# Streaming encoder layer on one core: late weight units loaded whole instead of in halves

## The chip, the core and the metric

The kernel runs on 1 core of one Trainium2 chip. The core has five engines with instruction streams of their own: TensorE (PE, matmuls), VectorE (DVE), ScalarE (ACT), GpSimd (POOL) and SyncE (SP, which here only issues DMAs). Sixteen DMA engines move data between HBM and the on-chip memory. The metric is the device time of one execution in microseconds; less is better.

## The reference

One transformer-like layer for 640 tokens (512 prompt tokens, and 8 streams of 16 sample tokens), D = 2048, all in float32:

```
p  = x @ w_in                              # q, k, v and gates of two mixers
h  = LN1(alpha*x + (sigmoid(gA)*(yA@w_proj_a) + sigmoid(gB)*(yB@w_proj_b)) @ w_out)
q  = h @ w_query                           # 8 heads, product keys, top 16 of 128 x 128
y  = LN2(alpha*h + sum_k gate_k * gelu(u[e_k] . h) * v[e_k])   # PEER, 16384 experts
```

`yA` and `yB` are two kinds of band attention. The part that matters here is PEER. The tables `u` and `v` are 16384 x 2048 floats each.

## The kernel before

**Weights as units.** Every stationary matrix is cut into units of 128 x 2048 floats (1 MB) that stand one behind another in `wstream`. SP loads unit n into `raw[n % 2]`; there are two such buffers. To keep float32 accuracy a unit is split: `w_hi` is the unit rounded to the matmul's format, and `w_lo = raw - w_hi`. PE then computes three products for each pair of tiles (high x high, low x high, high x low).

**Two stages.** Up to unit U_LATE the split is made by POOL alone and each unit is loaded whole (`raw_full`). The 240 units from U_LATE on, which this text calls late, are split in halves of 1024 columns: ACT rounds a half (`split_high`, L1024 to L1027), POOL subtracts it (`low`, L325 to L330), and each half is also loaded by a DMA of its own (L308 to L320).

**The order of one late unit n** (buffer s = n % 2). ACT's first half of `w_hi[s]` waits until PE has read the first half of unit n - 2 (`half_read`, or `part_done` where the unit holds `v`), and until the half has landed. POOL's `low` of half 0 raises `low_first`; its `low` of half 1 raises `split_done`. Between and behind the two lows POOL issues the gathers that are written out for this position. ACT's second half waits for the end of unit n - 2 on PE (`unit_done`).

**SP's queue.** It is in order. Half 0 of unit n + 2 may be loaded when `low_first` says that half 0 of unit n has been read, and half 1 when `split_done` says so for half 1.

**Where the halves are used.** 384 tokens go through PEER densely on PE: for each group of 4 x 128 experts, 4 units of `u` (`act_step`, L642), gelu, times the gate matrix, then 4 units of `v` (`out_units`, L706), whose results DVE adds into `r_acc` (L1439). The other 256 tokens go through PEER sparsely: POOL gathers 128 rows of 8 KB (1 MB, L365) from `u_rows` or `v_rows` into one of four buffers, and DVE multiplies and sums them (L1412, L1415), then frees the buffer (`rows_used`, which POOL waits for at L358 and L359). 16 early units of `u` come before U_LATE, and their results are kept in HBM.

**Trips.** First run 4 mixed trips, each with 12 late units (4 of `u`, 8 of `v`), 32 gathers and two loads of gates; then 24 late groups of 8 units, 16 gathers and one load of gates. A load of gates (L1031, issued by ACT) brings 768 KB of the gate matrix into `G4`; DVE's `product` (L1425) of the group waits for it. DVE works in program order: a product that waits holds back the gathered rows behind it, and so POOL's next gathers.

**Queues.** SP's loads run on DMA queue 1, POOL's gathers on queue 0, ACT's loads of gates on queue 10.

The functions that the change touches, and what calls them:

Of the kernel before, what the change touches and what calls it, by code (L numbers as in the profile page):

```python
# [50 lines left out]
U_LATE = U_PEER + N_EARLY  # L51
HALVES = (slice(0, D // 2), slice(D // 2, D))
# [30 lines left out]
def build(nc, x_t, wstream, u_rows, v_rows, cka, cva, ckb, cvb, rext, negs, bp_b, bs_b, sinks, lnp, lnrow, subk, consts, pt_out, y_out, n_out):  # L83
# [3 lines left out]
    ds = bass.ds  # L87

    with ExitStack() as ctx:
# [3 lines left out]
        def sb(name, shape, dt=f32):  # L93
            return ctx.enter_context(nc.sbuf_tensor(name, shape, dt))

        def sem(name):
            return ctx.enter_context(nc.semaphore(name))
# [9 lines left out]
        raw = [sb(f"w_raw{s}", [P, D]) for s in range(2)]  # L107
# [95 lines left out]
        def cut(ap, h):  # L203
# [10 lines left out]
                      lambda z, h=h: banks[:, 2 * z + h, 0:HALF]) for h in range(2)],  # L214
# [5 lines left out]


        raw_full = [sem(f"raw_full{s}") for s in range(2)]
        raw_half = [[sem(f"raw_half{s}_{h}") for h in range(2)] for s in range(2)]
        half_read, low_first = sem("half_read"), sem("low_first")
        hi_done, hi_late, split_done, unit_done = sem("hi_done"), sem("hi_late"), sem("split_done"), sem("unit_done")

# [72 lines left out]
        @block.sync  # L299
        def _(sp):  # L300
            for s in range(2):
                sp.dma_start(raw[s][:, :], wstream[s]).then_inc(raw_full[s], 16)
            with sp.Fori(1, U_LATE // 2) as i:
                for s in range(2):
                    sp.wait_ge(split_done, 2 * i + s - 1)
                    sp.dma_start(raw[s][:, :], wstream[ds(2 * i + s, 1)].rearrange("a p c -> p (a c)")) \
                        .then_inc(raw_full[s], 16)
            for s in range(2):  # L308
                sp.wait_ge(split_done, U_LATE - 1 + s)
                for h, half in enumerate(HALVES):  # L310
                    sp.dma_start(raw[s][:, half], wstream[U_LATE + s][:, half]).then_inc(raw_half[s][h], 16)
            with sp.Fori(1, (UNITS - U_LATE) // 2) as i:
                for s in range(2):
                    for h, half in enumerate(HALVES):
                        if h == 0:
                            sp.wait_ge(low_first, 2 * i + s - 1)
                        else:
                            sp.wait_ge(split_done, U_LATE - 1 + 2 * i + s)
                        sp.dma_start(raw[s][:, half], wstream[ds(U_LATE + 2 * i + s, 1), :, half].rearrange("a p c -> p (a c)")) \
                            .then_inc(raw_half[s][h], 16)  # L320


        @block.gpsimd
# [438 lines left out]
        def _(act):  # L762
# [204 lines left out]
            with act.Fori(0, N_QUERY // 2) as i:  # L967
                for s in range(2):
                    c = 2 * i + s
# [53 lines left out]

            def split_high(s, pair, h):  # L1024

                act.wait_ge(raw_half[s][h], 16 * pair + 16)
                act.activation(w_hi[s][:, HALVES[h]], raw[s][:, HALVES[h]], ACT.Copy).then_inc(hi_late, 1)  # L1027

            def load_gates(g, q):
# [13 lines left out]
            def act_units(g, q, first):  # L1043
                load_gates(g, q)
                for e in range(EG):
                    act.wait_ge(half_read, 4 * (g - EARLY) + e + 1)
                    split_high(e % 2, (first - U_LATE) // 2 + 1 + e // 2, 0)
                    act.wait_ge(unit_done, first + e + 1)
                    act.activation(banks[:, e, 0:N2], banks[:, e, 0:N2], ACT.Gelu).then_inc(gelu_done, 1)
                    split_high(e % 2, (first - U_LATE) // 2 + 1 + e // 2, 1)  # L1050
                    high_part(q, e, 0, banks[:, e, 0:N2])

            def out_unit(q, first, v):
                act.wait_ge(part_done, 12 * q + 3 * v + 2)
                split_high(v % 2, (first - U_LATE) // 2 + 1 + v // 2, 0)
                act.wait_ge(unit_done, first + v + 1)
                split_high(v % 2, (first - U_LATE) // 2 + 1 + v // 2, 1)
# [64 lines left out]
        def _(dve):  # L1122
# [127 lines left out]
            def layer_norm(q, between=None):  # L1250
                wide = [(cols, [out(z) for z in range(2)]) for (src, cols, out) in ln_parts[q]]
                dve.wait_ge(ln[q]["sum"], 1)
                for cols, out in wide:
                    last = dve.tensor_scalar(mean_t[:, cols], out[0], 1.0 / D, None, ALU.mult)
                own.done(last)
                own.wait()
                parts = ln_parts[q] if q else [(lambda k: Rt[:, k, :], slice(0, T), None)]
                for k in range(KT_N):
                    for (src, cols, _) in parts:
                        last = dve.tensor_tensor(src(k), src(k), mean_t[:, cols], ALU.subtract)  # L1260
                    last.then_inc(ln[q]["centered"], 1)
                if between:
                    between()
                dve.wait_ge(ln[q]["sq_used"], KT_N)
                for cols, out in wide:
                    last = dve.tensor_scalar(rstd_t[:, cols], out[1], 1.0 / D, EPS, ALU.mult, ALU.add)
                last.then_inc(ln[q]["var"], 1)
                dve.wait_ge(ln[q]["std"], 1)
                own.done(dve.reciprocal(rstd_t[:, cols], rstd_t[:, cols]) if q else dve.reciprocal(rstd_t, rstd_t))
                own.wait()  # L1270
                dve.wait_ge(ln[q]["centered"], KT_N)
                for k in range(KT_N):
                    for (src, cols, _) in parts:
                        last = dve.scalar_tensor_tensor(src(k), src(k), lnt[:, 2 * KT_N * q + k:2 * KT_N * q + k + 1],
                                                        rstd_t[:, cols], ALU.mult, ALU.mult)
                    last.then_inc(ln[q]["scaled"], 1)
                    if q == 0 and k:
                        split_shifted(k - 1)
# [371 lines left out]
```

## Time and profile before

| what | us |
| --- | --- |
| median of 3 runs | 4903.42 |
| lowest, highest | 4902.08, 4904.24 |
| the profiled execution, its own time | 4904.37 |
| its span, first to last instruction | 4902.6 |
| PE busy | 4388.6 |
| POOL busy | 2597.2 |
| DVE busy | 2675.2 |
| mean granted TensorE clock | 0.959 |

The profiled execution took 4904.37 us, of which 4902.6 us is the span that the rows below are measured in. Busy time is a sum over the whole program, whose stages differ.

### The profile page before, as it was taken

How to read it: one execution, taken by the hardware profiler on the slowest of the kernel's cores; microseconds unless marked ns; L12 is line 12 of the kernel's file. 1: busy time of each engine (PE TensorE's matmuls, PEld its weight loads, DVE VectorE, ACT ScalarE, POOL GpSimd, SP SyncE). 2: the span in 40 equal slices, each digit the busy share in tenths (PEclk: the TensorE clock that was granted, in tenths of full speed). 3: DMA queues.
4: the chain of work that ended last, by engine and by line, in shares of the span. 5: the costliest groups of instructions: out<-in, count | busy, mean ns of one | idle time of the engine just before them, and what ended most of it. 6: DMA issues, size and time to landing. Idle time of an engine off the chain costs nothing.

```text
span 4902.6 us, 74877 instructions
## 1 busy us (share of the span) xinstructions
PE 4388.6 (90%) x26508; PEld 4190.5 (85%) x26508; DVE 2675.2 (55%) x4819; ACT 1065.1 (22%) x1872; POOL 2597.2 (53%) x1718
## 2 busy tenths in 40 slices
PE   8999999999899989858867887999989999999996
PEld 8999888888799979857767777898889899998985
DVE  1000333344423138988966666766667667666667
ACT  1000222222311011012222222222223323322222
POOL 4454222232254534433266665767767777777673
PEclk9999999999999999979988989999999999999998
DMA  5222232222332321113478888889889899898895
GB/s 195 98 96 101 107 124 106 93 80 82 121 119 102 101 71 52 68 53 142 163 305 345 342 326 346 347 332 357 341 343 367 334 362 358 340 356 345 327 355 225
DMA packets 265955, 1081.84 MB, mean 221 GB/s; under 512 B 24496, under 2 KB 89136, under 8 KB 181168
## 3 DMA queue, kind: packets, MB, share of 16 engines
q0 software_dynamic: 74736, 544.24, 27.7%
q1 hardware_dynamic: 87840, 388.01, 21.7%
q10 hardware_dynamic: 103328, 148.96, 8.8%
q8 instruction: 25, 0.41, 0.0%
q14 instruction: 26, 0.21, 0.0%
HBM read 1019.65 MB, written 66.85 MB: 222 GB/s over the span
## 4 chain that ended last, share of the span: by engine, by line
PE 50%; DMA 17%; DVE 14%; issue 12%; POOL 5%; ACT 1%; DVEq 1%; ACTq 1%; POOLq 0%
PE banks L464 28%; PE banks L706 13%; DMA work<-gate_matrix 8%; DMA rows_own<-in_v_rows,idx 3%; POOL w_lo L329 3%; DMA rows_own<-in_u_rows,idx 2%; DVE banks L1415 2%; PE banks L642 2%; DMA work<-in_u_rows,idx 2%; POOL work L365 2%; PE banks L694 2%; PE banks L533 2%; PE banks L495 1%; DVE work L1412 1%; PE banks L503 1%
## 5 line engine op out<-in xcount | busy, mean ns | idle before, releaser
L329 POOL TENSOR_TENSOR w_lo<-w_raw,w_hi 128x1024 fp32r<-128x1024 f32 x480 | 1159.1, 2415 | 373.2 <-ACT w_hi L1027 367.5
L335 POOL TENSOR_SCALAR w_hi<-w_raw 128x2048 fp32r<-128x2048 f32 x130 | 253.5, 1950 | 1485.6 <-PE banks L464 1270.0
L464 PE MATMUL banks<-mv_hi,w_hi 128*128 128x256 f32 x3648 | 864.1, 318 | 61.9 <-DVE mv_lo L1134 38.0
L706 PE MATMUL banks<-mv_hi,w_hi 128*128 128x384 f32 x2048 | 723.5, 353 | 212.5 <-DVE work L1439 135.7
L464 PE MATMUL banks<-mv_lo,w_hi 128*128 128x256 f32 x3648 | 836.8, 311 | 0.0
L464 PE MATMUL banks<-mv_hi,w_lo 128*128 128x256 f32 x3648 | 835.6, 310 | 0.0
L642 PE MATMUL banks<-mv_hi,w_hi 128*128 128x384 f32 x2048 | 704.6, 344 | 77.8 <-POOL w_lo L329 61.7
L464 PEld LDWEIGHTS banks<-mv_hi,w_hi 128*128 128x128 f32 x3648 | 652.5, 189 | 125.9 <-issue 102.3
L1027 ACT ACTIVATE w_hi<-w_raw 128x1024 fp32r<-128x1024 f32 x480 | 506.2, 1057 | 968.7 <-PE banks L706 764.3
L706 PE MATMUL banks<-mv_lo,w_hi 128*128 128x384 f32 x2048 | 711.6, 347 | 0.0
L706 PE MATMUL banks<-mv_hi,w_lo 128*128 128x384 f32 x2048 | 710.5, 347 | 0.0
L642 PE MATMUL banks<-mv_lo,w_hi 128*128 128x384 f32 x2048 | 692.3, 338 | 0.0
L642 PE MATMUL banks<-mv_hi,w_lo 128*128 128x384 f32 x2048 | 691.8, 338 | 0.0
L339 POOL TENSOR_TENSOR w_lo<-w_raw,w_hi 128x512 fp32r<-128x512 f32 x520 | 679.2, 1337 | 10.9
L464 PEld LDWEIGHTS banks<-mv_lo,w_hi 128*128 128x128 f32 x3648 | 670.2, 190 | 0.0
L464 PEld LDWEIGHTS banks<-mv_hi,w_lo 128*128 128x128 f32 x3648 | 669.5, 189 | 0.0
L706 PEld LDWEIGHTS banks<-mv_hi,w_hi 128*128 128x128 f32 x2048 | 405.1, 198 | 241.2 <-DVE work L1439 149.7
L1415 DVE SCALAR_TENSOR_TENSOR banks<-work,subkt,banks 128x2048 f32<-128x2048 f32 x192 | 451.1, 2349 | 275.2 <-DMA work<-gate_matrix 234.4
L1412 DVE CUSTOM_DVE_ANT_0 work<-work,banks 128x2048 f32<-128x2048 f32 x192 | 438.2, 2282 | 242.8 <-DMA work<-gate_matrix 136.1
L642 PEld LDWEIGHTS banks<-mv_hi,w_hi 128*128 128x128 f32 x2048 | 391.0, 191 | 88.4 <-POOL w_lo L329 50.9
L706 PEld LDWEIGHTS banks<-mv_lo,w_hi 128*128 128x128 f32 x2048 | 405.9, 198 | 0.0
L706 PEld LDWEIGHTS banks<-mv_hi,w_lo 128*128 128x128 f32 x2048 | 405.0, 198 | 0.0
(159 smaller groups left out, 4825.5 us busy)
## 6 DMA issues: line engine op xcount, KB each, us to landing
w_raw<-in_wstream SPq DMA_DIRECT2D x480, 512.0 KB
w_raw<-in_wstream SPq DMA_DIRECT2D x130, 1024.0 KB, 4.8
gate_matrix<-work ACTq DMA_DIRECT2D x12, 2048.0 KB, 6.3
work<-gate_matrix ACTq DMA_DIRECT2D x32, 768.0 KB
out_p<-work ACTq DMA_DIRECT2D x34, 320.0 KB, 2.2
work<-out_p ACTq DMA_DIRECT2D x34, 320.0 KB, 3.4
gate_scratch<-work ACTq DMA_DIRECT2D x32, 320.0 KB, 2.2
work<-gate_scratch ACTq DMA_DIRECT2D x16, 640.0 KB, 3.9
```

The source lines that it names most:

```text
L329: pool.tensor_tensor(w_lo[s][:, part], raw[s][:, part], w_hi[s][:, part].bitcast(f32), ALU.subtract) \
L335: pool.tensor_scalar(w_hi[s][:, :], raw[s][:, :], 1.0, 0.0, ALU.mult, ALU.add).then_inc(hi_done, 1)
L339: last = pool.tensor_tensor(w_lo[s][:, part], raw[s][:, part], w_hi[s][:, part].bitcast(f32), ALU.subtract)
L365: pool.indirect_dma_start(rows_t[c % ROWS], None, table, bass.IndirectOffsetOnAxis(ap=idx2[:, c % 16:c % 16 + 1], axis=0)) \
L464: last = pe.matmul(acc(dst, h), a[s][:, P * k:P * k + P], b[h][:, k, :], start=(k == k_first and n == 0), stop=(k == k_last and n == 2))
L533: last = pe.matmul(o, v_nat[:, P * kb + HD * hh:P * kb + HD * hh + HD], pt[:, P * c:P * c + P], start=(c == 0), stop=(c == nk - 1))
L642: last = pe.matmul(banks[:, bank, 0:N2], a[s][:, P * k:P * k + P], b[1][:, k, :], start=(k == 0 and n == 0), stop=(k == KT_N - 1 and n == 2))
L694: last = pe.matmul(banks[:, 2 + q % 2, P * t:P * t + P], oh2[:, n, :].bitcast(f32), oh1[:, n, :], start=True, stop=True)
L706: last = pe.matmul(banks[:, d, 0:N2], a[v % 2][:, at:at + P], b[z][:, e, :], start=(e == 0 and n == 0), stop=(e == EG - 1 and n == 2))
L1027: act.activation(w_hi[s][:, HALVES[h]], raw[s][:, HALVES[h]], ACT.Copy).then_inc(hi_late, 1)
L1412: ins = dve.tensor_tensor_reduce(rows, rows, nat, 1.0, 0.0, ALU.mult, ALU.add, dots[:, c:c + 1])
L1415: ins = dve.scalar_tensor_tensor(nat, rows, act_n[:, ds(col + c, 1)], nat, ALU.mult, ALU.add)
```

## The change

SP issues one DMA of 1 MB for each late unit, where it issued two of 512 KB. The one DMA waits for `split_done`; SP no longer waits for `low_first`, which PE still uses. The two semaphores of a buffer's halves become one, `raw_late`, and both halves of ACT's rounding wait for it. Rounding, subtraction and what they release stay in halves. The first two late units are loaded whole too.

```
-        raw_half = [[sem(f"raw_half{s}_{h}") for h in range(2)] for s in range(2)]
+        raw_late = [sem(f"raw_late{s}") for s in range(2)]
...
             for s in range(2):
                 sp.wait_ge(split_done, U_LATE - 1 + s)
-                for h, half in enumerate(HALVES):
-                    sp.dma_start(raw[s][:, half], wstream[U_LATE + s][:, half]).then_inc(raw_half[s][h], 16)
+                sp.dma_start(raw[s][:, :], wstream[U_LATE + s]).then_inc(raw_late[s], 16)
             with sp.Fori(1, (UNITS - U_LATE) // 2) as i:
                 for s in range(2):
-                    for h, half in enumerate(HALVES):
-                        if h == 0:
-                            sp.wait_ge(low_first, 2 * i + s - 1)
-                        else:
-                            sp.wait_ge(split_done, U_LATE - 1 + 2 * i + s)
-                        sp.dma_start(raw[s][:, half], wstream[ds(U_LATE + 2 * i + s, 1), :, half].rearrange("a p c -> p (a c)")) \
-                            .then_inc(raw_half[s][h], 16)
+                    sp.wait_ge(split_done, U_LATE - 1 + 2 * i + s)
+                    sp.dma_start(raw[s][:, :], wstream[ds(U_LATE + 2 * i + s, 1)].rearrange("a p c -> p (a c)")) \
+                        .then_inc(raw_late[s], 16)
...
             def split_high(s, pair, h):
 
-                act.wait_ge(raw_half[s][h], 16 * pair + 16)
+                act.wait_ge(raw_late[s], 16 * pair + 16)
                 act.activation(w_hi[s][:, HALVES[h]], raw[s][:, HALVES[h]], ACT.Copy).then_inc(hi_late, 1)
```

On SP, in the loop over the late units (one pass is two units, one for each buffer), stood before the change and stand now, with the semaphore that a row waits for:

```order
-L319 ISA [waits low_first]
-L319 DMA w_raw<-in_wstream 128x1024
...
-L319 ISA [waits split_done]
-L319 DMA w_raw<-in_wstream 128x1024
-L319 ISA [waits low_first]
-L319 DMA w_raw<-in_wstream 128x1024
-L319 ISA [waits split_done]
-L319 DMA w_raw<-in_wstream 128x1024
...
+L314 ISA [waits split_done]
+L314 DMA w_raw<-in_wstream 128x2048
+L314 ISA [waits split_done]
+L314 DMA w_raw<-in_wstream 128x2048
```

The transfer that waited for `low_first` is gone, and its 1024 columns moved into the one behind `split_done`. No instruction of PE, DVE, ACT or POOL moves.

## Rows read from the trace of the kernel before

**Rows 1.** Windows by stage: length, engines' busy time, clock, DMA share, GB/s

```profile
2467.00:3110.00 643.00, 501.61 (x2607) 489.65 (x2608) 436.60 (x485) 139.76 (x169) 414.54 (x273) 0.89 0.88 338
3110.00:4840.00 1730.00, 1592.61 (x8834) 1566.27 (x8833) 1130.74 (x1072) 484.20 (x572) 1245.59 (x787) 0.98 0.90 347
```

**Rows 2.** PE's groups of instructions from 2467 to 4840 us

```profile
L706 PE MATMUL banks<-mv_hi,w_hi 128*128 128x384 f32 x2021 | 714.4, 353 | 212.5 <-DVE work L1439 135.7 <-DVE mv_lo L1429 76.6
...
L642 PE MATMUL banks<-mv_hi,w_hi 128*128 128x384 f32 x1792 | 608.4, 339 | 74.2 <-POOL w_lo L329 61.7 <-DVE work L1439 12.5
```

**Rows 3.** Chain that ended last, one late group: start, us, what

```profile
4032.56 13.27 DMA work<-gate_matrix
...
4056.37 8.00 DMA work<-in_u_rows,idx
...
4066.99 8.94 DMA rows_own<-in_u_rows,idx
...
4078.76 19.03 PE banks L706 x108
```

**Rows 4.** Windows of that group and of a mixed trip: columns as in rows 1

```profile
4063.00:4089.00 26.00, 21.59 (x122) 20.64 (x121) 19.94 (x24) 7.71 (x9) 22.02 (x16) 1.00 1.01 415
2643.00:2647.00 4.00, 4.00 (x25) 4.00 (x24) 4.00 (x7) 2.80 (x4) 3.83 (x3) 1.00 1.00 418
2639.00:2641.00 2.00, 2.00 (x14) 2.00 (x13) 2.00 (x1) 0.00 (x0) 1.17 (x2) 1.00 0.00 0
4046.00:4050.00 4.00, 4.00 (x25) 4.00 (x24) 3.98 (x3) 0.00 (x0) 0.94 (x2) 1.00 0.02 8
2641.00:2682.00 41.00, 31.21 (x164) 30.25 (x163) 32.66 (x35) 9.49 (x14) 27.35 (x19) 0.91 0.99 399
2720.00:2728.00 8.00, 5.02 (x20) 5.02 (x21) 7.12 (x10) 2.42 (x3) 4.94 (x3) 0.61 0.18 42
```

**Rows 5.** Timeline of SP, narrow windows: start, us, issue of a half

```profile
2635.86 0.33 SPq L319 DMA_DIRECT2D w_raw<-in_wstream  x1
2645.51 0.33 SPq L319 DMA_DIRECT2D w_raw<-in_wstream  x1
4041.32 0.33 SPq L319 DMA_DIRECT2D w_raw<-in_wstream  x1
4052.82 0.33 SPq L319 DMA_DIRECT2D w_raw<-in_wstream  x1
4056.38 0.33 SPq L319 DMA_DIRECT2D w_raw<-in_wstream  x1
4059.93 0.33 SPq L319 DMA_DIRECT2D w_raw<-in_wstream  x1
```

**Rows 6.** DMA queue 1 in 2636:2639, 4044:4046: packets, MB, share

```profile
q1 hardware_dynamic: 143, 0.52, 51.8%
...
q1 hardware_dynamic: 131, 0.49, 66.6%
```

**Rows 7.** Page, DMA issues: size, median us from issue to landing

```profile
w_raw<-in_wstream SPq DMA_DIRECT2D x130, 1024.0 KB, 4.8
```

**Rows 8.** Timelines of ACT and POOL after the gates have landed

```profile
4063.42 1.05 ACT L1027 ACTIVATE w_hi<-w_raw 128x1024 fp32r<-128x1024 f32 x1
...
4066.72 1.06 ACT L1027 ACTIVATE w_hi<-w_raw 128x1024 fp32r<-128x1024 f32 x1 [0.72 <-DMA w_raw<-in_wstream]
...
4067.97 2.41 POOL L329 TENSOR_TENSOR w_lo<-w_raw,w_hi 128x1024 fp32r<-128x1024 f32 x1
4070.54 0.96 POOL L365 DMA_INDIRECT work<-in_u_rows,idx  x1 [0.16 <-issue]
```

**Rows 9.** Timeline of DVE, same stretch

```profile
4080.02 2.28 DVE L1412 CUSTOM_DVE_ANT_0 work<-work,banks 128x2048 f32<-128x2048 f32 x1
```

**Rows 10.** DMA queues from 3200 to 4800 us: packets, MB, share of 16 engines

```profile
q0 software_dynamic: 49287, 358.87, 56.2%
q1 hardware_dynamic: 48814, 177.73, 30.2%
```

## Prediction

> **What bounds the kernel now.** I read the windows by stage first [rows 1]. Before 2467 us only whole units are used and the change touches next to nothing. From there to 4840 us run the 240 late units, with the DMA engines 0.88 to 0.90 busy. In the mixed trips (643 us) PE is busy for only 502 us; in the late groups (1730 us) for 1593 us, so there PE is nearly the bound. What PE waits for stands in its groups [rows 2]: 212.5 + 74.2 = 286.7 us of idle time, of which 148.2 us end with DVE's addition into `r_acc` (L1439), 76.6 us with DVE's low part of the products (L1429), and 61.7 us with POOL's subtraction. No row there names the weight load itself. So the question is not whether PE waits for a load, but what delays DVE and POOL.
>
> The chain that ended last tells that for one late group [rows 3]. The load of gates takes 13.27 us from issue to landing; DVE stands still meanwhile. Then two gathers follow, 8.00 us and 8.94 us from issue to use, and only then PE starts its long run at 4078.76. Each of these is a transfer that shares the 16 DMA engines. Behind the landing the engines are full (4063:4089: share 1.01, 415 GB/s [rows 4]). Only right after it they are idle (4046:4050: 8 GB/s), since DVE has freed no buffer yet and POOL has issued no gather. In a mixed trip it is the same picture, longer: idle at 2639:2641, then 0.99 busy for 41 us. So behind each landing of gates runs a chain whose length is bytes divided by the rate, and PE's stalls end with it.
>
> **The change, part by part.**
>
> *Bytes and instructions.* The bytes stay. SP issues 240 DMAs fewer (0.33 us each), on a queue that nothing else uses and that mostly waits: no gain. The packets of a load grow from 4 KB to 8 KB. In the full windows a mixture of 4 KB packets and 8 KB gathers moves 415 GB/s (4063:4089), gathers alone 418 GB/s (2643:2647) [rows 4]: I price packet size at 0. The nearest row for the other end is the share that each queue's packets took [rows 10]: queue 0 moves 358.87 MB at 56.2%, so queue 1 at that rate would need 27.8% for its 177.73 MB and has 30.2%. 2.4% of the DMA-bound stretches (about 100 of 158 us in each of 4 trips, about 23 of some 72 us, 1730 / 24, in 24 groups, 950 us) is 23 us, the upper bound of a gain.
>
> *The first half leaves later.* It was allowed out after POOL's first low of unit n, now after the second. In a stretch where POOL is not stopped that is 3.5 us later (4056.38 to 4059.93 [rows 5]). But where the gates are awaited, POOL is stopped between the two lows, by a gather whose buffer DVE has not freed: 4041.32 to 4052.82, and 2635.86 to 2645.51 [rows 5]. In the mixed trip the half issued at 2635.86 moved its 0.52 MB in 2636:2639 [rows 6], at a time when no gather was under way, free of charge. Now these bytes are issued at 2645.5, into the full stretch. They lengthen it by 0.52 MB / 0.415 MB per us = 1.26 us. Two landings of gates in each of 4 trips give 8 x 1.26 = **10 us**. Other pauses of the gathers in a trip, as 2720:2728 at 42 GB/s [rows 4], could lose as much, up to 2 more a trip, 10 us; but there DVE waits for its own small loads and PE's next stall begins before the engines are full again, so I take 0 for these.
>
> *The same in a late group.* Here the half issued at 4041.32 overlaps the gates: in 4044:4046 queue 1 moved 0.49 MB [rows 6]. Behind the landing the count up to the chain's second gather, at 4075.9, was 5 1/3 halves (second half of one unit, two units, a third of the next first half); now it is 3 whole units, 6 halves, since the next is issued only after 4074. 2/3 of 0.52 MB is 0.35 MB, 0.85 us longer. Against that the gates land earlier, since that half is no longer among their rivals, while the unit before it is loaded later and gives part of this back; I take 0.5 us of the 1.1 us that 0.49 MB are worth. Net 0.35 us, with ends 0 - 0.25 and 0.85. For 24 groups: **8 us**, ends -6 and 20.
>
> *Is a whole load in time?* Uncontended, 1 MB takes 4.8 us [rows 7], of which 1.05 MB / 0.418 = 2.5 us is moving, so 2.3 us is fixed. Sharing turn by turn with one gather doubles the moving: 2.3 + 5.0 = 7.3 us. The tightest place is the load issued at 4059.93: it would land at 4067.2, where ACT's first half of it was rounded at 4063.42 and the second at 4066.72, the latter already 0.72 us late [rows 8]. Rounding then ends at 4068.3, and POOL's low, which began at 4067.97 because POOL was busy until then, slips by 0.4 us; the next unit by about 0.8. POOL's gathers behind it slip alike. The one issued at 4070.54 [rows 8] is used by DVE at 4080.02 without any wait [rows 9], 9.5 us later, against 8.0 and 8.9 us for the ones in the chain. So 0.4 to 0.8 us is hidden by that queueing time. Price 0. Away from the landings POOL follows PE, a unit every 8.4 us, and the load has about 8.7 us to ACT's first half: also hidden. If this cover were gone, each group would pay the slip.
>
> *Sum.* 4904.4 (this execution's own time) + 10 + 8 = **4922 us**. The profiled execution is 1 us over the median of the runs, 4903.4; I keep 4922.
>
> **The skill on large transfers.** The rows show that a whole load of 1 MB takes 4.8 us alone [rows 7], and that PE's waits name no load [rows 2]. The Trainium skill, page "DMA: Bandwidth & Descriptors", section "Bandwidth", has the rule to batch DMAs to 1 MiB and more, and gives about 2.0 us of fixed cost for each plus the bytes at 436 GB/s; by that two halves cost 6.4 us and one whole 4.4 us, an estimate, and 240 units would give back 480 us if loads were on the path. The rule is for transfers that are waited for one by one; here the trace speaks against a gain of that size, since two halves overlap other transfers.
>
> **Rivals.**
> 1. *Larger packets win* (faster). If the 2.4% of rows 10 is true engine time and the idle-time bytes are recovered in the slack of the steady stretches (0.90 busy on average), the 23 us stand against about 8: 4904 - 15 = 4889. For it: the shares of rows 10. Against: equal rates in the full windows. It decides where windows with whole loads move over 4% more than 415 GB/s.
> 2. *It cancels* (no change). The half that was free in idle time is lost, but the gates' load has fewer rivals and the gathers ahead of the chain fewer bytes to share with; the two terms shrink to 0 to 8 us: 4904 to 4912. For it: in late groups my own net is only 0.35 us out of terms of 0.5 and 0.85.
> 3. *The load is late* (slower still). If a contended whole load takes 9.5 us, 2.2 more than worked out, the slip is 2.6 us and then about 5 at the next unit, past the 1 us or so that queueing hides; gathers and then PE move by about 2 us in each group, 48 us, and the sum is 4970. For it: ACT's second half is already 0.72 us late. Against: 7.3 us is already the case with a gather beside it all the way. It decides from about 8.5 us.
>
> **How the numbers follow.** My forecast (4913 to 4940) gets 0.42, the cancelling 0.31, larger packets 0.14, late loads 0.13. The bounds of the terms alone give 4904 - 6 - 23 = 4875 to 4904 + 20 + 20 = 4944; to leave out no more than 0.2, the range goes from 4892 to 4955. My forecast's own range is 4908 to 4940. 0.2% is 9.8 us, about what a measurement of this kernel tells from no change: faster means under 4893.6, slower over 4913.2. Faster 0.14; within 0.31; slower 0.55.
>
> **What the profile afterwards would show.** (a) The load behind the one that stalls now, near 4041, is issued only when POOL's second low ends, and the DMA engines are idle for longer after each landing of gates, 1 to 2 us more. (b) The mixed stage, 643 us, is about 10 us longer, the late one, 1730 us, about 8. (c) The chain still runs gates, two gathers, PE, with gathers of 8 to 10 us. (d) ACT's wait for `w_raw` is more frequent, once or twice a group, under 1 us at the second half's old place, at most 4 at the first's; POOL's wait for ACT grows, PE's for POOL's subtraction does not. (e) Full windows stay near 415 GB/s. The prediction is wrong if (e) fails upward, if whole loads under contention take over 8.5 us, or if PE's idle time behind L1439 does not grow.

## The result and the profile after

| kernel | median us | lowest to highest | runs |
| --- | --- | --- | --- |
| before | 4905.31 | 4894.05 to 4914.35 | 16 |
| changed | 4875.93 | 4855.65 to 4903.25 | 15 |

The ratio is 0.994, with a 95% interval of 0.9927 to 0.9953: the change makes the kernel 29 us or 0.6% **faster**, where 4922 us was predicted. (Executions far off all others, of 11954.88 us here and of 7710.94 and 7067.46 us of the kernel before in later runs, are left out.) Besides the median the spread moved: 20 us before, 48 us now. The profiled execution of the changed kernel is the slowest of its 15, 4903.25 us, so its trace shows what the change does to the transfers and hardly any of the gain. For the gain I ran the same kernel again (first experiment). All lines from L324 on stand five lower than before: L1434 is what L1439 was.

Windows by stage of the changed kernel [rows 1]: length, busy time of PE, PEld, DVE, ACT and POOL, clock, DMA share, GB/s.

```profile
2469.00:3112.00 643.00, 506.27 (x2629) 493.44 (x2630) 436.51 (x488) 140.15 (x170) 417.41 (x275) 0.89 0.87 339
3112.00:4840.00 1728.00, 1578.62 (x8818) 1549.87 (x8817) 1131.66 (x1070) 483.88 (x571) 1244.37 (x785) 0.98 0.89 347
```

PE's groups of the same stretch [rows 2]:

```profile
L701 PE MATMUL banks<-mv_hi,w_hi 128*128 128x384 f32 x2023 | 710.5, 351 | 231.1 <-DVE work L1434 129.4 <-DVE mv_lo L1424 101.6
L637 PE MATMUL banks<-mv_hi,w_hi 128*128 128x384 f32 x1792 | 607.1, 339 | 63.4 <-POOL w_lo L324 60.6 <-DVE work L1434 2.8
```

The chain that ended last, one late group [rows 3], its long pieces:

```profile
4031.23 13.70 DMA work<-gate_matrix
...
4066.09 9.63 DMA rows_own<-in_u_rows,idx
```

Windows of that group [rows 4]: behind the landing of the gates, and the full stretch after it.

```profile
4045.00:4050.00 5.00, 5.00 (x31) 5.00 (x30) 4.89 (x5) 0.00 (x0) 1.83 (x3) 1.00 0.00 0
4051.00:4069.00 18.00, 17.29 (x98) 16.65 (x97) 13.37 (x16) 6.92 (x11) 15.63 (x11) 1.00 0.99 395
```

The view of SP's line of late loads, x238: who waited for them (us, times), and the time to landing.

```profile
  ACT w_hi L1022: 448.1, 123
...
DMA to landing us min/median/max: 4.6/8.9/11.0
```

DMA queue 1 from 3200 to 4800 us [rows 10]:

```profile
q1 hardware_dynamic: 24340, 177.24, 28.9%
```

Read together: half as many packets on queue 1 for the same bytes, and 28.9% of the engines' time for them instead of 30.2%; an idle stretch of 5 us behind the landing, and a full one at 395 GB/s, not above the 415 of before. The idle stretch is no longer than it was: before, it stands one microsecond later.

```profile
4046.00:4051.00 5.00, 5.00 (x31) 5.00 (x30) 4.98 (x6) 0.00 (x0) 1.92 (x3) 1.00 0.09 16
```

ACT now waits for weights 123 times, 3.6 us each in the mean. And yet PE waits no longer for POOL's subtraction: 60.6 against 61.7 us. In this one execution nothing is won either: it is within 2 us of the kernel before.

### The profile page after: what moved, and what is told of

Read it like the earlier page. It is cut to its first block, busy times and chain, and to the rows that moved or that the text cites. A ratio compares the mean times of both kernels' runs of the same rounds, so it can differ in the third digit from the quotient of the medians.

```text
span 4901.5 us, 74042 instructions
## 1 busy us (share of the span) xinstructions
PE 4380.2 (89%) x26508; PEld 4179.1 (85%) x26508; DVE 2677.4 (55%) x4819; ACT 1065.6 (22%) x1872; POOL 2598.5 (53%) x1718
## 4 chain that ended last, share of the span: by engine, by line
PE 49%; DMA 17%; DVE 14%; issue 12%; POOL 6%; ACT 1%; DVEq 1%; ACTq 0%; POOLq 0%
PE banks L459 28%; PE banks L701 12%; DMA work<-gate_matrix 8%; POOL w_lo L324 4%; DMA work<-in_u_rows,idx 2%; DMA rows_own<-in_u_rows,idx 2%; DMA rows_own<-in_v_rows,idx 2%; DVE banks L1410 2%; PE banks L637 2%; POOL work L360 2%; PE banks L689 2%; PE banks L528 2%; PE banks L490 1%; DMA work<-in_v_rows,idx 1%; DVE work L1407 1%
## 5 line engine op out<-in xcount | busy, mean ns | idle before, releaser
L324 POOL TENSOR_TENSOR w_lo<-w_raw,w_hi 128x1024 fp32r<-128x1024 f32 x480 | 1158.2, 2413 | 367.1 <-ACT w_hi L1022 361.8
L637 PE MATMUL banks<-mv_hi,w_hi 128*128 128x384 f32 x2048 | 704.7, 344 | 67.1 <-POOL w_lo L324 60.6
## 6 DMA issues: line engine op xcount, KB each, us to landing
work<-gate_matrix ACTq DMA_DIRECT2D x32, 768.0 KB, 14.3
```

The source lines that it names most:

```text
L324: pool.tensor_tensor(w_lo[s][:, part], raw[s][:, part], w_hi[s][:, part].bitcast(f32), ALU.subtract) \
L637: last = pe.matmul(banks[:, bank, 0:N2], a[s][:, P * k:P * k + P], b[1][:, k, :], start=(k == 0 and n == 0), stop=(k == KT_N - 1 and n == 2))
```

## Experiments

Each kernel was timed in five rounds against the kernel before on the same chip. Medians of before were 4905 to 4912 us, so the ratios are what is compared; a difference between two kernels is the difference of their ratios times 4904.

| run | median us | ratio | 95% interval |
| --- | --- | --- | --- |
| whole_again | 4868.11 | 0.9916 | 0.9885 to 0.9946 |
| halves_at_second_low | 4889.94 | 0.9965 | 0.9952 to 0.9979 |
| whole_in_trips | 4892.2 | 0.9967 | 0.995 to 0.9984 |
| whole_in_groups | 4874.98 | 0.9944 | 0.9922 to 0.9966 |
| gates_in_6kb_halves | 4798.29 | 0.9781 | 0.9759 to 0.9803 |
| gates_in_6kb_halves_at_second_low | 4789.42 | 0.9758 | 0.9737 to 0.9778 |
| gates_in_6kb_whole | 4763.31 | 0.9708 | 0.9688 to 0.9729 |
| gates_6kb_one_dma_4kb | 4764.28 | 0.97 | 0.9676 to 0.9723 |
| gates_6kb_one_dma_8kb_copy | 4753.49 | 0.9673 | 0.9648 to 0.9698 |
| one_dma_4kb | 4879.54 | 0.9943 | 0.9916 to 0.9971 |
| whole_as_two_dmas | 5524.12 | 1.1252 | 1.1228 to 1.1276 |
| whole_as_four_quarters | 5119.77 | 1.0437 | 1.0413 to 1.0462 |
| early_acts_sooner_halves | 4876.79 | 0.9941 | 0.9925 to 0.9957 |
| early_acts_sooner_halves_late | 4879.95 | 0.9936 | 0.992 to 0.9952 |
| early_acts_sooner_one_dma_4kb | 4864.1 | 0.99 | 0.9868 to 0.9933 |
| early_acts_sooner_whole | 4852.81 | 0.9886 | 0.9867 to 0.9905 |
| gates_6kb_whole_early_acts_sooner | 4751.58 | 0.9677 | 0.9655 to 0.9699 |

Two lengths are used below, both of the profiled execution and both from the issue times of the gates' loads on ACT: *trips* is from the first load to the ninth (the four mixed trips), *group* the mean distance from the ninth to the 32nd, over 23. *DVE for gates* adds the two rows of who waited for those loads.

| run | span | trips | group | DVE for gates |
| --- | --- | --- | --- | --- |
| before | 4902.6 | 584.6 | 75.10 | 370.5 |
| changed, the execution above | 4901.5 | 583.6 | 75.02 | 367.3 |
| whole_again | 4835.1 | 564.2 | 73.23 | 313.1 |
| halves_at_second_low | 4884.5 | 569.9 | 75.18 | 370.5 |
| one_dma_4kb | 4852.8 | 556.7 | 74.18 | 327.7 |
| gates_in_6kb_halves | 4796.5 | 581.1 | 70.65 | 257.0 |
| gates_in_6kb_whole | 4764.3 | 546.1 | 70.72 | 243.2 |
| gates_in_6kb_halves_at_second_low | 4787.7 | 566.9 | 70.86 | 249.3 |
| gates_6kb_one_dma_4kb | 4760.9 | 548.2 | 70.66 | 225.3 |

### The same kernel again

No edit; the changed kernel as it is.

> The changed kernel once more, for its time and for a second profiled execution, since the first profiled execution took 4903 us where the median of the others was 4876 us. Theory A (the larger packets use the DMA engines better): about 4876 us, and in the profile the full windows move more than 415 GB/s. Theory B (the later issue leaves the engines to the gates and the gathers): about 4876 us, with a shorter wait for the gates. If the first profiled execution was only at the slow end of a wide spread, this one is likely to be nearer 4876 us and shows in which stage the time is saved.

Measured: 0.9916, and its profiled execution took 4836.88 us, near the low end of its own spread (4833.49 to 4888.35). The chain that ended last, two groups of it:

```profile
3401.75 7.85 DMA work<-gate_matrix
...
3430.99 10.05 DMA rows_own<-in_v_rows,idx
...
3444.13 25.26 PE banks L701 x144
...
3469.85 14.87 DMA work<-gate_matrix
...
3506.06 9.32 DMA rows_own<-in_v_rows,idx
...
3518.47 26.54 PE banks L701 x144
...
3545.48 8.00 DMA work<-gate_matrix
```

The first load of gates lands in 7.85 us, and the next group begins 68.1 us later; the second takes 14.87 us, and its group 75.6 us. Nothing else in the chain differs by as much. Of the 24 late groups seven have such a landing here, of 7.5 to 8.1 us; in the execution shown above none has, its shortest being 9.3 and 10.3 us. (Three groups, the first, ninth and seventeenth, lie between the two lengths in both.) The two rows of who waited for the gates say what it is worth; of before and of this run:

```profile
  DVE banks L1415: 234.4, 16
  DVE work L1412: 136.1, 10
```

```profile
  DVE banks L1410: 195.4, 16
  DVE work L1407: 117.7, 10
```

57.4 us less waiting. L1415 and L1412 are DVE's steps on gathered rows. In the code DVE's wait for the gates (`act_units` on DVE) stands ahead of the group's first two such steps, which do not read the gates; what that order costs was not tried.

The gates are 768 KB in 1536 packets of 512 bytes. DMA queues (packets, MB, share of 16 engines) in the first group at 3406:3408, and in the second at 3475:3477 and 3477:3479:

```profile
q10 hardware_dynamic: 1074, 0.55, 94.8%
q0 software_dynamic: 17, 0.03, 4.2%
...
q10 hardware_dynamic: 739, 0.38, 65.4%
q0 software_dynamic: 48, 0.27, 32.3%
...
q1 hardware_dynamic: 52, 0.43, 54.9%
q0 software_dynamic: 35, 0.28, 33.7%
q10 hardware_dynamic: 254, 0.13, 25.4%
```

With the other queues empty the gates rush through, over 500 packets a microsecond. Once gathers and weights are back, as in the changed kernel at 4039:4042, each queue gets about as many packets as the other, and the gates a few:

```profile
q1 hardware_dynamic: 76, 0.62, 50.0%
q0 software_dynamic: 74, 0.61, 48.6%
q10 hardware_dynamic: 47, 0.02, 2.8%
```

The packets take turns singly: of the 47 packets of gates 26 are followed, within 3 ns of their end, by the start of a gather's packet and only 6 by another of the gates; by chance it would be 8 and 5. At 16 packets of 512 bytes a microsecond what is left of the gates crawls until the others stop. So the landing has two lengths. That the short one comes where the gap lasts some 3 us, 1536 packets at 500 a microsecond, is my reading of these windows.

### One stage at a time

Of whole_in_trips, with `N_CUT` = 25 (the end of the trips); whole_in_groups has the two bodies the other way round:

```
+            with sp.Fori(1, N_CUT) as i:
+                for s in range(2):
+                    sp.wait_ge(split_done, U_LATE - 1 + 2 * i + s)
+                    sp.dma_start(raw[s][:, :], wstream[ds(U_LATE + 2 * i + s, 1)].rearrange("a p c -> p (a c)")) \
+                        .then_inc(raw_half[s][0], 16)
+                    sp.sem_inc(raw_half[s][1], 16)
-            with sp.Fori(1, (UNITS - U_LATE) // 2) as i:
+            with sp.Fori(N_CUT, (UNITS - U_LATE) // 2) as i:
```

> Whole loads for the 50 units of the mixed trips alone, halves in the late groups. It divides the gain of some 29 us between the stages. Theory A (packets): the gain is in proportion to the time in which the DMA engines are full, about 100 of 158 us in each of 4 trips against 23 of 75 us in 24 groups, so about 12 us of the 29 are here: 4893 us. Theory B (later issue): it goes by landings of gates, 8 of 32, so about 7 us: 4898 us.

> Halves in the mixed trips, whole loads in the late groups alone. Theory A (packets): about 17 us of the 29, 4888 us. Theory B (later issue): about 22 us, 4883 us. Either way this and the run with whole loads in the trips should add up to the whole gain; if they do not, the stages act on one another.

Measured: -16 us and -27 us, whose sum of 43 us is that of whole_again (-41 us), though the first measurement of the whole change gave 29 us. The gain is in both stages. In the profiled executions whole_in_trips has 578.0 and 74.81 us (trips, group), whole_in_groups 591.8 and 73.55.

### The deferral alone

```
                         if h == 0:
-                            sp.wait_ge(low_first, 2 * i + s - 1)
-                        else:
                             sp.wait_ge(split_done, U_LATE - 1 + 2 * i + s)
```

Still two loads of 512 KB in 4 KB packets, both at the second low. This is the step that the prediction priced at 10 + 8 us.

> Two loads of 512 KB as before, but both issued at the end of the second low, when the changed kernel issues its one of 1 MB. This is the later issue alone, with 4 KB packets. Theory A (packets): no faster than before, 4905 us or, if the later issue costs what the prediction said, about 4922 us. Theory B (later issue): about 4876 us like the changed kernel.

Measured: 0.9965, **17 us faster**, in a narrow spread (4886 to 4898). Its group is as long as before, its trips 15 us shorter. Where these come from shows in a mixed trip of the kernel before: timeline of SP, ACT, DVE and POOL, each asked in a window of its own.

```profile
2707.49 0.33 SPq L319 DMA_DIRECT2D w_raw<-in_wstream  x1
...
2708.03 0.93 ACTq L1040 DMA_DIRECT2D work<-early_act  x2
...
2716.54 0.56 DVE L1425 TENSOR_TENSOR work<-work 128x384 f32<-128x384 f32 x1 [5.95 <-DMA work<-early_act]
2720.76 0.56 DVE L1425 TENSOR_TENSOR work<-work 128x384 f32<-128x384 f32 x1 [3.67 <-DMA work<-early_act]
...
2722.90 2.38 POOL L329 TENSOR_TENSOR w_lo<-w_raw,w_hi 128x1024 fp32r<-128x1024 f32 x1 [10.42 <-ACT w_hi L1027]
```

A half goes out half a microsecond ahead of two small loads (192 KB each) for which DVE then stands still 9.6 us. The window of rows 4 at 2720:2728, 42 GB/s, is the end of this: ACT's next rounding stands in its order behind what it makes of DVE's two products, POOL's low waits 10.42 us for that rounding, and the gathers behind the low stop. DVE's whole wait for these loads, before, with the halves deferred, and in whole_again:

```profile
  DVE work L1425: 33.9, 8
```

```profile
  DVE work L1423: 17.9, 8
```

```profile
  DVE work L1420: 22.9, 7
```

### These waits taken away

ACT issues the two small loads ahead of the third output unit instead of behind it:

```
-                out_unit(2 * i, first + EG, 2)
                 for e in range(2, 4):
                     load_act(i, q, e, 8 * i + 7 + e - 2)
+                out_unit(2 * i, first + EG, 2)
```

> The kernel before, but ACT issues the last two loads of early activations of a mixed trip (192 KB each) about 4.7 us sooner, ahead of the rounding of the next unit's first half. Theory D: in the mixed trips the halves loaded at the first low collide with these small loads, for which DVE waits 5.9 and 3.7 us in a trip, while everything else stands still; whole loads, issued later, leave them a free stretch. If they are issued sooner their waits go for halves too: some 4 us for each of the 4 trips, so about 4890 us. If these waits cost nothing in the end, the time stays at 4908 us.

> The changed kernel with the same two loads issued sooner. Theory D: the part of the gain that comes in the mixed trips (16 us) is mostly had already by the sooner loads, so whole against halves gives less than before, 12 to 20 us (the short landings of gates in the late groups) instead of 29 to 40: about 4870 us. If the later issue gains in another way, whole loads keep their whole lead: about 4855 us.

> The kernel before with the small loads of early activations issued sooner (4876.8 us), and now also with both halves of the weights issued at the second low. What the deferral of the first half does is here seen without the waits for early_act that it shortens. If the deferral by itself costs as the prediction had it (1.26 us for each landing of gates in the trips, 0.35 us in a group, 18 us in all), this run is at 4895 us (4885 to 4905). If it costs nothing and all of its 17 us of gain came from the shorter waits, it is at 4877 us (4870 to 4883). Below 4870 us the deferral gains by more than these waits.

> The same early issue of the small loads, the weights as one load of 4 KB packets at the second low, gates in 512 byte packets. One load of 8 KB packets was at 4852.8 us here. If it is one load in place of two that gives the clear run of 3.4 us, this run is at 4853 to 4866 us with some landings of gates under 9 us, and at least 10 us below the run with two halves; if it is the packets' size, it is within 5 us of the run with two halves.

Measured: in halves 0.9941, which is 29 us from an edit that touches no weights, and more than the 15 us or so that I had expected. Deferring both halves on top of it gives 0.9936, the same within the intervals: once the waits for early_act are gone, the deferral neither gains nor costs (-2 us, about +-11). Its trips are 559.6 against 557.7 us. So the 17 us were these waits, and the 18 us of cost that I had computed are not there. The whole load keeps a lead of 27 us over the halves here (0.9886 against 0.9941), so its lead does not rest on these waits alone, and one load of 4 KB packets keeps 18 us over the deferred halves (0.99 against 0.9936); that last pair's intervals overlap.

### The gates in 6 KB packets

The gate matrix is stored in HBM as [group, partition, block, expert x token], so that a load of gates has 128 packets of 6 KB instead of 1536 of 512 bytes. The 12 stores that write the matrix, ahead of the late units, are laid out to match (not shown); each takes 9.1 us to land instead of 6.3.

```
-        G_s = dram("gate_matrix", (GBLK, P, KEYS, GT))
+        G_s = dram("gate_matrix", (GROUPS, P, GBLK, EG * GT))
...
-                act.dma_start(G4.rearrange("p b e t -> p b (e t)"),
-                              G_s[:, :, ds(EG * g, EG), :].rearrange("b p e t -> p b (e t)")).then_inc(g4_in, 16)
+                act.dma_start(W2[:, 2 * N2:6 * N2],
+                              G_s[ds(g, 1)].rearrange("a p b c -> p (a b c)")).then_inc(g4_in, 16)
```

> The kernel before, with the gate matrix laid out in HBM so that a load of gates is 128 runs of 6 KB (8 packets for each DMA engine) instead of 1536 runs of 512 bytes (96 for each); weights in halves as before. Theory C, from the profiles so far: a load of gates is served one packet for each packet of the other queues, so it ends only in a moment when gathers and weights are both drained; whole loads open such a moment now and then, the load of gates then lands in 7 to 8 us instead of 14 to 15, and the group takes 67 us instead of 75. With 8 packets it needs no such moment: landing after 5 to 9 us in every group, about 7 us less for each of 30 loads, so about 4700 us. Theory A (packet size of the weights): the wait for the gates goes by bytes, which are the same, so about 4905 us.

> The changed kernel with the same layout of the gate matrix. Theory C: as fast as with the weights in halves, about 4700 us, less at most the 16 us of the later issue in the mixed trips; the gain of whole loads in the late groups, 27 us, is gone, and the spread of the times is as small as before. Theory A: the 29 us between whole and half stay, wherever the total lies.

> Gates in runs of 6 KB, and both halves issued at the second low. Halves at their old places with these gates took 4798 us, whole loads 4763 us, and the 35 us between them lie in the mixed trips. If they come from the time of issue (theory D), this run takes 4763 to 4775 us; if from the size of the packets, about 4798 us.

Measured: I had expected about 4700 us with halves, and it is 4798. The landing has one length, but not the 5 to 9 us that I had counted on; the row of the gates' load in gates_in_6kb_halves:

```profile
DMA to landing us min/median/max: 4.1/9.9/10.9
```

In halves this takes 107 us off the kernel before, almost four times what the change studied here gives. A group is 70.65 us with halves and 70.72 with whole loads: with the gates in large packets for both, **the change gains nothing in the groups**. Its gain there was the chance of a short landing. The spread went with it in these two runs, 15 and 12 us over five executions; the later kernels with 6 KB gates and one load spread over 24 to 27 us, so the spread has another part that is not explained. In the trips the gain stays, and is larger (581.1 to 546.1); all in all the ratio still falls from 0.9781 to 0.9708, 36 us, of which the deferral gives 11 us (0.9758, between my two expectations) and the rest 25 us.

### What the rest is: packets of 8 KB, or one load instead of two

Two first tries split the whole load again, at the same low. Of whole_as_two_dmas, whose packets stay 8 KB:

```
-                    sp.dma_start(raw[s][:, :], wstream[ds(U_LATE + 2 * i + s, 1)].rearrange("a p c -> p (a c)")) \
+                    for p in (slice(0, P // 2), slice(P // 2, P)):
+                        sp.dma_start(raw[s][p, :], wstream[ds(U_LATE + 2 * i + s, 1), p].rearrange("a p c -> p (a c)")) \
```

> The whole unit at the end of the second low, as two DMAs of 64 partitions each with packets of 8 KB. It tells the number of DMAs from the size of the packets: the halves at the second low were two DMAs with packets of 4 KB and took 4890 us. If the packets count (theories A and C): about 4870 us, with landings of gates in under 10 us in some of the late groups. If the number of DMAs counts: about 4890 us and hardly any.

> The whole unit at the end of the second low, as four DMAs of 512 columns with packets of 2 KB. With packets taken in turns with the gathers a load then takes 32 turns of an engine instead of 8, so the weight queue is hardly ever empty beside gathers. Theory C: no short landing of gates in the late groups, and loads land later (over 10 us beside gathers), so that POOL waits: 4890 us or more. If only the time of issue counted, about 4890 us as with halves, and the same landings.

Both failed as tests. The two loads of 64 partitions each made the kernel 12.5% slower. Its DMA records from 3200 to 4700 us, and those of whole_again:

```profile
DMA packets 81382, 409.90 MB, mean 273 GB/s; under 512 B 8313, under 2 KB 32889, under 8 KB 32889
...
q0 software_dynamic: 36553, 266.22, 59.7%
q1 hardware_dynamic: 19990, 131.01, 31.9%
```

```profile
DMA packets 102736, 537.82 MB, mean 359 GB/s; under 512 B 8288, under 2 KB 39008, under 8 KB 39008
```

The engines were no less busy (95.0% against 92.1% with queue 10's 3.4% and 3.7%), at three quarters of the rate. Four quarters of 512 columns (2 KB packets, four loads) cost 4.4%, with ACT waiting 1474.2 us for weights; that changes size and number at once. My expectation for the number of short landings missed too: half of its groups had one.

Then one load with packets of 4 KB, from a second input `wlate` of the late units, laid out as [unit, half, partition, 1024]; a control has that second input with packets of 8 KB.

```
-                    sp.dma_start(raw[s][:, :], wstream[ds(U_LATE + 2 * i + s, 1)].rearrange("a p c -> p (a c)")) \
+                    sp.dma_start(raw[s][:, :].rearrange("p (h c) -> p h c", h=2),
+                                 wlate[ds(2 * i + s, 1)].rearrange("a h p c -> p (a h) c")) \
```

> The changed kernel, but a late unit's 1 MB comes from a copy of the weights laid out so that its one load has packets of 4 KB where the changed kernel's has 8 KB; one issue, one wait, the same bytes at the same second low. If it is the packets that give the whole load its further 24 us over two halves issued together (4889.9 us), this kernel is at about 4890 us (4880 to 4900), the load takes about 7.5 us from first to last packet beside the gathers (whole in 8 KB packets 5.3 us), and next to none of the gates' loads of the late groups lands in under 9 us. If it is the number of loads (two issues on SyncE against one), it is at about 4870 us (4855 to 4880), with packets of 4 KB or not, and the load takes as long as that of the changed kernel.

> The gates in packets of 6 KB, which takes the chance of the short landings away, and a late unit's 1 MB as one load of 4 KB packets from a second copy. With gates in 6 KB two halves at the second low took 4789.4 us and one load of 8 KB packets 4763.3 us, both in narrow spreads. If the 26 us between them are the packets' size, this run is at 4789 us (4783 to 4795); if they are the number of loads, at 4763 us (4757 to 4770); in between both have a part.

> The control for the run with 4 KB packets: the same second input for the late units, but laid out as before, so that the one load has packets of 8 KB. Both theories expect 4763 us (4757 to 4770), the time of one load of 8 KB packets from the first input. If this run is elsewhere, where the copy lies in HBM has a price of its own and the other run must be read against this one.

Measured: with the gates in 512 bytes it came out between the two expectations, 4879.5 us in a wide spread of 4831 to 4902, with landings of gates under 9 us in six groups, and did not tell. With the gates in 6 KB one load of 4 KB packets is at 0.97, like one of 8 KB packets (0.9708, and 0.9673 from the copy), while two loads are at 0.9758. That points to **the number of loads**, 28 us by 0.9758 to 0.97. But the control came out 17 us below the same load from the first input, where I had expected no difference, and I had said that the 4 KB run must then be read against it. If the copy's place in HBM is really worth 17 us, 11 us are left for the number of loads and 13 us are the packets' size (0.97 to 0.9673). The intervals of these last two differences overlap, so neither is settled. Against a price of the place speaks that the packets took as long from either input, in the mean of the late groups' records: 178 ns (two loads) and 176 ns (one, from the copy) for 4 KB, 338 and 341 ns for 8 KB. So the number of loads is worth 11 to 28 us, more likely the upper end.

In the profiled executions 18.7 us of it lie in the trips (566.9 to 548.2). DVE's wait for the small loads of early_act is 14.0 us shorter there, which is most of it; with two loads and with one:

```profile
  DVE work L1423: 24.4, 8
```

```profile
  DVE work L1421: 10.4, 5
```

How one load differs from two stands in a group of each. Two loads, gates in 6 KB: timeline of SP and POOL, then the DMA queues in 3774:3775, 3776:3777 and 3778:3781.

```profile
3772.57 0.33 SPq L317 DMA_DIRECT2D w_raw<-in_wstream  x1
3773.09 0.70 SPq L317 DMA_DIRECT2D w_raw<-in_wstream  x1
...
3772.55 0.96 POOL L363 DMA_INDIRECT rows_own<-in_u_rows,idx  x1 [0.16 <-issue]
...
q1 hardware_dynamic: 69, 0.28, 106.1%
...
q0 software_dynamic: 43, 0.35, 89.3%
q1 hardware_dynamic: 11, 0.01, 6.8%
...
q0 software_dynamic: 116, 0.82, 64.8%
q1 hardware_dynamic: 125, 0.45, 36.4%
```

One load of 4 KB packets, at the same place of the program, and the queues in 3748:3750 and 3751:3753:

```profile
3746.30 0.96 POOL L361 DMA_INDIRECT rows_own<-in_u_rows,idx  x1 [0.16 <-issue]
3746.32 0.37 SPq L314 DMA_DIRECT2D w_raw<-in_wlate  x1
...
q1 hardware_dynamic: 185, 0.76, 93.1%
...
q0 software_dynamic: 96, 0.79, 92.7%
```

Weights and a gather are issued at the same moment in both. As one load the weights pass before the gather's packets come, and the gather then has the engines to itself. As two, the second half's packets come after the gather's first ones and have to share with them. Taken one by one, 23 of the 188 late loads of the groups land in under 5 us in this run, 24 in one_dma_4kb, 30 in the copy with 8 KB and 29 in whole_again; of the units of halves_at_second_low whose landing the trace has, 94, none is complete within 8 us of its first issue. In the trips of this run it is 9 of 50 loads. That these clear runs are what shortens the trips, by leaving the small loads a free stretch, is the reading that fits; no run here switches them off by themselves.

### All together

The change, the gates in 6 KB and the small loads sooner:

> The version that the runs point to: whole loads, gates in runs of 6 KB, and the early activations loaded sooner. With whole loads and 6 KB gates DVE still waits 12 us in all for early activations, so at most that is to be had: 4750 to 4763 us, faster than every kernel so far.

Measured: 0.9677 (4751.58 us), 158 us under the kernel before and the fastest median of the study, though the copy of the weights with gates in 6 KB alone is level with it (0.9673).

## Why the prediction was wrong

The direction was wrong: 4922 us, at least 4892, against 4876. In short, I counted bytes in full stretches, and the time lay in waits of DVE: in the trips for two small loads, which get through sooner when the halves leave later or as one, and in the groups for the gates, which now and then land in half the time. Step by step:

- **"The first half leaves later", 10 us in the trips: failed.** The step read the half issued in an idle stretch as free, and its deferral as bytes added to a full one. The deferral alone made the kernel 17 us faster. The step left out what else is in flight where the half goes: elsewhere in each trip that is two small loads for which DVE waits. I had read the window 2720:2728 and taken 0 for it, because "there DVE waits for its own small loads", and did not ask what delays those. Without these waits it costs nothing that the runs can tell (-2 us, about +-11).
- **"The same in a late group", 8 us: failed.** A group with deferred halves is 75.18 us long, before 75.10: the 0.08 us are nothing, where 0.35 was said. With the whole load a group has either the old length or one some 7 us shorter, through the gates; the groups alone gave 27 us. I had treated the 13.27 us of the gates as a fixed length, less 0.5 us for fewer rivals. The rows of the trace held what was needed: 768 KB at 415 GB/s is 1.9 us, and a landing of 13 us must be waiting its turn.
- **"Price packet size at 0": nearly right for the rate, and beside the point.** The shown full window moves 395 GB/s, and (e) held. But the same step passed over the number of loads: "240 DMAs fewer", it said, no gain. That term measures 11 to 28 us; it lies not in SP's issue times but in when the second load's packets arrive.
- **"Is a whole load in time?" held in its conclusion, not its numbers.** I worked out 7.3 us contended; the median is 8.9, over the 8.5 from which rival 3 was to decide. ACT waits 448.1 us for weights instead of 26.7. It costs nearly nothing: from 3110 to 4700 POOL's wait for ACT is 181.5 us in whole_again, 167.3 before, and PE's for POOL, from 2467 us on, fell from 61.7 to 50.7. So rival 3, the late load, did not come.
- **Rival 1**, larger packets, had the right side and 4889 us, with the wrong mechanism. It was to show in full windows more than 4% above 415 GB/s; the fullest 26 us of the late groups moved 420 GB/s before (3682:3708) and 423 in whole_again (3798:3824). Of its 2.4 points of engine time 1.3 came (30.2% to 28.9%), and the execution that shows them gained nothing.
- **Rival 2**, that it cancels, had 4904 to 4912 us. Like my forecast it looked at the gates' rivals, but took their landing as one length that shrinks by a little.
- Of what the profile was to show, (a) failed in the group shown, where the engines are idle for 5 us before and after, and held in the trips (2639.5:2644.5 of the changed kernel is empty; in 2636:2639 of before stood the half). (b) was wrong in sign. (c) held for the gathers' length, but one gather, not two, is in the chain shown, the other's place being taken by POOL's lows. (d) was wrong in size: 53 of ACT's 123 waits are over 4 us. Two of my three signs of being wrong came: loads over 8.5 us, and PE's idle time behind L1439 not growing (148.2 us before, 132.2 in the changed kernel's rows, 117.0 in whole_again).

The Trainium skill, page "DMA: Bandwidth & Descriptors", section "Bandwidth", which I had set aside, wants few large DMAs. The fixed cost for each, which the same page has in the section "Anatomy of one DMA — SWDGE (gpsimd) path", would have given 480 us if loads were waited for one by one, an estimate; it stands there for transfers that GpSimd issues. The direction was right, and the runs show 11 to 28 us of it.

## What to carry to other kernels

Where transfers share the engines, ask for each wait for a transfer whose packets it stands behind, and how many packets it needs to get through: a load that takes 13 us for 2 us worth of bytes is a layout to be changed, and here was worth almost four times the change. Before pricing a moved transfer by its bytes, list every load that is in flight at the old and at the new place. And when the spread of times grows with a change, compare executions from both ends of it for a wait that has two lengths.

## What was not expected of the hardware

- A load of many 512 byte packets starves beside loads of large ones: 16 packets a microsecond with both other queues busy, over 500 alone. The same 768 KB in 128 packets of 6 KB lands in 9.9 us in the median (gates_in_6kb_halves) instead of 14.3 (the changed kernel's page; the trace of before lacks its landings).
- Two loads issued 0.5 us apart are not one load (3772.57 and 3773.09 above): the packets of the second can fall behind a gather that was issued before it and would have come after a single load.
- Loads to 64 partitions in 8 KB packets drag everything down to 273 GB/s at full engines, against 359. The Trainium skill, page "SBUF — State Buffer", section "Door 1: The DMA port swizzle", says that 64 neighbouring partitions reach only half of the 16 ports, and section "Can I just issue two DMAs to hit both halves?" that two such loads don't add up. The run agrees with the direction; it also shows the gathers of another queue slowed with them, 266.22 MB for 59.7% of the engines' time where whole_again moves 349.24 MB for 58.6%.
